# 42 tokens of the last dense tile fetch their experts' rows, where 32 did

## The reference

```python
s1, i1 = lax.top_k(s[:, :, 0], 16); s2, i2 = lax.top_k(s[:, :, 1], 16)      # 8 heads, 128 keys each side
best, pos = lax.top_k(s1[..., None] + s2[..., None, :], 16)                 # 16 experts of a head
gate = softmax(best)
act = einsum('td,thkd->thk', h, expert_u[idx])                              # 8 x 16 = 128 experts a token
out = einsum('thk,thkd->td', gate * gelu(act), expert_v[idx])
```

## Time and profile before

| what | value |
|---|---|
| median of 3 runs | 4116.03 us |
| profiled execution | 4116.04 us, span 4114.3 us |
| PE, PE's weight loads busy | 99%, 90% |
| DVE, ACT, POOL busy | 53%, 34%, 59% |
| experts' units | from about 2058 us |
| value units | from about 3099 us |
| DMA | 929 MB, mean 226 GB/s |

### The profile page before, as it was taken

How to read it: one execution, slowest core, us unless ns; L and a number is a source line. 1 busy time by engine, 2 the same in 40 slices (tenths; PEclk the granted TensorE clock), 3 DMA queues, 4 the chain that set the end, 5 groups by cost and what they waited for, 6 DMA issues and landing times.

```text
span 4114.3 us, 54344 instructions
## 1 busy us (share of the span) xinstructions
PE 4067.4 (99%) x21875; PEld 3688.9 (90%) x21875; DVE 2170.0 (53%) x2854; ACT 1401.8 (34%) x1756; POOL 2420.6 (59%) x768
## 2 busy tenths in 40 slices
PE   8999999999999999999999999999999999999998
PEld 7888888877877888888899999999999999999997
DVE  4300035121122011207888888888437888888885
ACT  4322222332333121223345555555332222232233
POOL 4444443433433434443357777777778888888883
PEclk9999999999999999999999999999999999999999
DMA  4233322222222433323248999999989999999993
GB/s 184 94 123 121 117 102 94 97 82 82 93 82 82 163 115 115 118 92 133 92 165 331 346 345 344 346 347 344 366 340 384 398 381 384 382 385 381 390 364 133
DMA packets 210813, 929.39 MB, mean 226 GB/s; under 512 B 18672, under 2 KB 96816, under 8 KB 111408
## 3 DMA queue, kind: packets, MB, share of 16 engines
q1 hardware_dynamic: 64080, 460.35, 30.4%
q0 software_dynamic: 46080, 335.56, 20.8%
q10 hardware_dynamic: 100576, 132.56, 9.0%
HBM read 864.41 MB, written 64.00 MB: 226 GB/s over the span
## 4 chain that ended last, share of the span: by engine, by line
PE 93%; POOL 2%; DVE 2%; ACT 1%; DMA 1%; issue 1%; ACTq 0%; SPq 0%; DVEq 0%; POOLq 0%
PE bank L1952 16%; PE bank L1953 15%; PE bank L1954 15%; PE bank L1992 8%; PE twin L1992 8%; PE bank L2296 4%; PE twin L2296 4%; PE twin L2298 4%; PE bank L2298 4%; PE twin L2297 4%; PE bank L2297 4%; POOL low L575 1%; PE twin L2267 1%; PE twin L1953 1%; PE twin L1954 1%
## 5 line engine op out<-in xcount | busy, mean ns | idle before, releaser
L575 POOL TENSOR_TENSOR low<-raw,high 128x2048 fp32r<-128x2048 f32 x351 | 1629.2, 4642 | 1447.4 <-ACT high L684 1263.4
L684 ACT ACTIVATE high<-raw 128x2048 fp32r<-128x2048 f32 x190 | 363.9, 1915 | 1220.6 <-PE bank L1954 737.7
L1952 PE MATMUL bank<-x_pack,high 128*128 128x352 f32 x1952 | 630.9, 323 | 8.6 <-POOL low L575 8.6
L1952 PE MATMUL bank<-x_high,high 128*128 128x512 f32 x1632 | 636.9, 390 | 0.0
L1954 PE MATMUL bank<-x_high,low 128*128 128x512 f32 x1632 | 635.0, 389 | 0.0
L1953 PE MATMUL bank<-x_low,high 128*128 128x512 f32 x1632 | 635.0, 389 | 0.0
L1953 PE MATMUL bank<-low_pack,high 128*128 128x352 f32 x1952 | 629.7, 323 | 0.0
L1954 PE MATMUL bank<-x_pack,low 128*128 128x352 f32 x1952 | 629.5, 323 | 0.0
L696 ACT ACTIVATE high<-raw 128x2048 fp32r<-128x2048 f32 x162 | 310.5, 1917 | 737.6 <-PE twin L2298 433.6
L1952 PEld LDWEIGHTS bank<-x_pack,high 128*128 128x128 f32 x1952 | 367.3, 188 | 10.7 <-issue 6.3
L1953 PEld LDWEIGHTS bank<-low_pack,high 128*128 128x128 f32 x1952 | 367.3, 188 | 0.0
(11 more groups left out here) (301 smaller groups left out, 7336.2 us busy)
## 6 DMA issues: line engine op xcount, KB each, us to landing
raw<-weights SPq DMA_DIRECT2D x353, 1024.0 KB
raw_values<-weights SPq DMA_DIRECT2D x42, 1024.0 KB
raw_experts<-weights SPq DMA_DIRECT2D x38, 1024.0 KB
act_dram<-act_out ACTq DMA_DIRECT2D x128, 176.0 KB
retrieved_dram<-stage ACTq DMA_DIRECT2D x44, 512.0 KB
act_in<-act_dram ACTq DMA_DIRECT2D x32, 704.0 KB
gates_in<-retrieved_dram ACTq DMA_DIRECT2D x32, 704.0 KB
gates_dram<-sgu_act ACTq DMA_DIRECT2D x32, 256.0 KB, 2.0
```

The source lines that it names most:

```text
L575: nc.gpsimd.tensor_tensor(low[:, slot, :], rounded, high[:, slot, :].bitcast(F32), ALU.subtract).then_inc(low_done, 1)
L684: nc.scalar.activation(high[:, slot, :], raw[:, slot, :], ACT.Copy).then_inc(high_done, 1)
L1952: nc.tensor.matmul(o, high[:, slot, w], xh, start=(k == 0), stop=False)
```

## The change

`EXTRA` goes from 32 to 42. A token's 128 slots no longer divide evenly: 3 parts of 43 slots, the 129th with gate 0, on 126 partitions; the last two partitions copy the first two of part 0. `EXTRA_GAP` 1 puts an extra row after each slot row, `LATE` goes to 15. The dense part has 342 columns, 86 gate steps, and 11 stages, of which the last has 6 steps and a piece stored after each of the first four. The product of activations and gates is done in two instructions, 10 full stages and 22 columns of the last. The divisor in `sums_by` is 7 units short of the end instead of 10.

```diff
-EXTRA = 32
+EXTRA = 42
-STAGES = COLS // STAGE_TOK
+STAGES = -(-COLS // STAGE_TOK)
+GATE_STEPS = -(-COLS // WTOK)
+LAST_STEPS = GATE_STEPS - STEPS * (STAGES - 1)
+TRAIL = ETILES - FIRST_STEP - GATE_STEPS
-EXTRA_ROWS = SLOTS // EXTRA_SLOTS
-LATE = 16
+EXTRA_ROWS = -(-SLOTS // EXTRA_SLOTS)
+EXTRA_USED = EXTRA_SLOTS * EXTRA
+EXTRA_LISTED = EXTRA_SLOTS * EXTRA_ROWS
+PAD = P - EXTRA_USED
+LATE = 15
-EXTRA_GAP = 2
+EXTRA_GAP = 1
...
-    return min(V_ROWS, early + max(0, unit - begin) * (V_ROWS - LATE) // (ETILES - 10 - begin))
+    return min(V_ROWS, early + max(0, unit - begin) * (V_ROWS - LATE) // (ETILES - 7 - begin))
...
-            act.dma_start(wide_extra[:], extra_x_dram.rearrange("j i d -> (j i) d")).then_inc(extra_x_in, 16)
+            act.dma_start(wide_extra[0:EXTRA_USED, :], extra_x_dram.rearrange("j i d -> (j i) d")).then_inc(extra_x_in, 16)
+            act.dma_start(wide_extra[EXTRA_USED:P, :], extra_x_dram[0, 0:PAD, :]).then_inc(extra_x_in, 16)
...
-                for q in range(STEPS):
+                n_steps, gap = (STEPS, 2) if after else (LAST_STEPS, 1)
+                for q in range(n_steps):
                     expert_unit(q % 2, index + q, high=ring_high)
-                    if before and q % 2 == 0:
-                        keep_stage(s - 1, 1 - half, q // 2)
+                    if before and q % gap == 0 and q // gap < PIECES:
+                        keep_stage(s - 1, 1 - half, q // gap)
...
-                act.dma_start(tile[:], dram.rearrange("j i g -> (j i) g")).then_inc(extra_in, 16)
+                act.dma_start(tile[0:EXTRA_USED, :], dram.rearrange("j i g -> (j i) g")).then_inc(extra_in, 16)
+                act.dma_start(tile[EXTRA_USED:P, :], dram[0, 0:PAD, :]).then_inc(extra_in, 16)
...
+            nc.vector.memset(extra_gates[:, SLOTS:EXTRA_LISTED], 0.0)
...
+            nc.vector.tensor_copy(extra_slots[:, SLOTS:EXTRA_LISTED],
+                                  extra_slots[:, 0:EXTRA_LISTED - SLOTS]).then_inc(extra_named, 1)
...
-                acts = act_in[:, slot, :, :].rearrange("p e (s t) -> p e s t", t=STAGE_TOK)
+                whole = (STAGES - 1) * STAGE_TOK
+                acts = act_in[:, slot, :, 0:whole].rearrange("p e (s t) -> p e s t", t=STAGE_TOK)
                 gates = gates_in[:, slot, :, :, :].rearrange("p s e t -> p e s t")
-                nc.vector.tensor_tensor(acts, acts, gates, ALU.mult).then_inc(product_done, 1)
+                nc.vector.tensor_tensor(acts, acts, gates[:, :, 0:STAGES - 1, :], ALU.mult)
+                acts = act_in[:, slot, :, whole:COLS]
+                nc.vector.tensor_tensor(acts, acts, gates[:, :, STAGES - 1, 0:COLS - whole],
+                                        ALU.mult).then_inc(product_done, 1)
```

More of the change, by code:

```diff
@@ L328, in program @@
         pos_half = c("pos_half", [P, 2, TT, P], U32)
[L329 to L330 removed]
+        extra_slots = at("extra_slots", [P, EXTRA_LISTED], U32, region_b)
+        extra_gates = at("extra_gates", [P, EXTRA_LISTED], F32, region_b + 1024)
         picked = at("picked", [P, P, TOPK], F32, region_b)
@@ L1177, in keep_stage @@
                 if n == 0:
-                    act.wait_ge(step_out, steps.next(STEPS))
+                    act.wait_ge(step_out, steps.next(STEPS if isinstance(s, int) and s < STAGES - 1 else LAST_STEPS))
                 kept_stages[half].next(16)
@@ L1190, in stage_units @@
                 index = s * STEPS + FIRST_STEP
-                for q in range(STEPS):
+                n_steps, gap = (STEPS, 2) if after else (LAST_STEPS, 1)
+                for q in range(n_steps):
                     expert_unit(q % 2, index + q, high=ring_high)
-                    if before and q % 2 == 0:
-                        keep_stage(s - 1, 1 - half, q // 2)
-                    if after or q < STEPS - 1:
+                    if before and q % gap == 0 and q // gap < PIECES:
+                        keep_stage(s - 1, 1 - half, q // gap)
+                    if after or q < n_steps - 1:
                         gate_parts((q + 1) % 2, s * STAGE_TOK + (q + 1) * WTOK)
@@ L1718, in _ @@
             nc.vector.memset(extra_pick[:], 0.0)
-            nc.vector.tensor_copy(extra_gates[:], all_best[:, DENSE_T - 1, :, :].rearrange("p h k -> p (h k)"))
-            nc.vector.scalar_tensor_tensor(out=extra_slots[:], in0=expert_i[:, 0, DENSE_T - 1, :], scalar=float(KEYS),
-                                           in1=expert_i[:, 1, DENSE_T - 1, :], op0=ALU.mult,
-                                           op1=ALU.add).then_inc(extra_named, 1)
+            nc.vector.memset(extra_gates[:, SLOTS:EXTRA_LISTED], 0.0)
+            nc.vector.tensor_copy(extra_gates[:, 0:SLOTS], all_best[:, DENSE_T - 1, :, :].rearrange("p h k -> p (h k)"))
+            then(nc.vector.scalar_tensor_tensor(out=extra_slots[:, 0:SLOTS], in0=expert_i[:, 0, DENSE_T - 1, :],
+                                                scalar=float(KEYS), in1=expert_i[:, 1, DENSE_T - 1, :], op0=ALU.mult,
+                                                op1=ALU.add))
+            nc.vector.tensor_copy(extra_slots[:, SLOTS:EXTRA_LISTED],
+                                  extra_slots[:, 0:EXTRA_LISTED - SLOTS]).then_inc(extra_named, 1)
             dve.wait_ge(gffn_in, 16)
-            dve.wait_ge(extra_x_in, 16)
+            dve.wait_ge(extra_x_in, 2 * 16)
             nc.vector.tensor_tensor(wide_extra[:], wide_extra[:], gffn_all[:], ALU.mult)
@@ L1814, in _ @@
                     dots += 1
-                if at_step < STAGES * STEPS:
+                if at_step < GATE_STEPS:
                     gate_sum(at_step)
@@ L2277, in _ @@
             gate_pair(first=True)
-            with repeat(pe, STAGES * STEPS // 2 - 1, *column_pair, (made, 2), (outs, 2)):
+            with repeat(pe, GATE_STEPS // 2 - 1, *column_pair, (made, 2), (outs, 2)):
                 gate_pair()
```

7 lines of the change are left out of this document (2 added, 5 removed).

## The result

The kernel after takes 4132.01 us (median of 8 runs, 4126.92 to 4138.9), the kernel before, on the same chip, 4118.03 (8 runs): a ratio of 1.003, 95% interval 1.002 to 1.0039. It is slower by 0.3%, where 4100 and a gain of 0.4% was forecast. The profiled execution took 4127.22 us, its span is 4125.5, 11.2 longer than that of before.

What follows compares the result with a forecast made beforehand. Matmul time on TensorE was taken as the bound (PE holds 93% of the chain of waits). -50.8 - 1.0 + 17.5 + 3 + 3 + 0.5 + 11.7 = -16.1 from 4116.03 gave 4100 us, range 4078 to 4120.

Steps and rivals of the forecast that it cites:

- Columns (-50.8): Both stages: 12192 matmuls, each 10 columns narrower, save 4.17 ns each by N + 32 cycles, -50.8 us in all.
- Rival (d): The change doesn't shorten a matmul, 342 columns being charged as 352: 4132 us, slower; chance 0.05.
- Gate steps (-1.0): Gate steps go from 88 to 86, saving two times 0.48 us of PE: -1.0 us.
- Extra rows (+17.5): Experts' stage: slow 2.75 us fetches beside dots with `wide_extra` delay `low`; PE waits 25.3 us against 7.8: +17.5.
- rival (b): Locks cascade: the 13 units with the extra first stall too, +17 more, 4117 us, no change; chance 0.16.
- late-held `low`: Experts' stage: in seven of twelve waits a lone extra's dot keeps `low` late, adding up to 1.25 us each.
- The restart near the end: Behind the wait near the end, TensorE restarts at 1.2 GHz, adding 1.7 us.
- Value stage (+3, +3, +0.5): Value stage: POOL's late `low` +3, late `values` at the entry +3, longer waits behind ACT's table loads +0.5 us.
- The entry: Start of the value stage: two rows a unit outrun the transfers, PE waits for `values`: +3 us (0 to +8).
- POOL's edge: Value stage: with two fetches the next `low` is 0.7 us late against 0.75 slack: +3 (0 to +12).
- Rival (c): Transfers become the value stage's bound, 384 GB/s being the ceiling: +35 us, so 4135, slower; chance 0.09.
- Sums with seven units to go (+11.7): Near the end: the later sum delays ACT's `high` and POOL's `low`; PE waits about 11.2 us, net +11.7.

Runs made afterwards that it cites:

- the bench: TensorE alone with no other work, rows of 96 or 192 matmuls per width in the kernel's order, nothing of the block computed; 342 columns took 157.8 ns at 1536 bytes.
- the lead of 348: Kernel after with 40 tokens (344 columns), extra row first, nine units to go; each experts' unit's first three matmuls take 348 columns: 4090.01 us, ratio 0.9933.

## Why the prediction was wrong

**Columns (-50.8): the step that failed.** "Ten columns are 4.17 ns": measured 2.45 in the experts' stage and 0.88 in the value stage, -20 us for -50.8. These 31 us are the miss: between the profiled executions -16.1 was forecast and +11.2 came, and the other terms, some too high and some left out, end 3 lower together. The bound named for it, 0, was taken for a charge of 342 as 352; that isn't what happened. "Three widths lie on one line" was true of the rows and no ground for a fourth: the bench has up to 5.7 ns more than N + 32 cycles (338) and up to 2.2 less (304), and 352 itself has 160.0 or 161.1 by what runs before it; behind four of 256, as in the kernel, it happens to be the 160.0 of the line. The placement adds to it: at 1368 bytes from row to row 342 columns cost 1.0 more than at the 1408 of before. Rival (d) gave 4132 and the time came out there by luck: it had the columns at nothing instead of -20 and the rows at +4 instead of +12.7, and no wait or clock beyond the forecast ones. Its chance of 0.05 shows how little the assumption was weighed: no row showed a width other than 256, 352 and 512.

**Gate steps (-1.0).** Two of 0.48 us are gone; no run shows them by themselves, they are inside the -13.9.

**Extra rows (+17.5).** Mechanism right: twelve long fetches beside the dot with `wide_extra`, twelve waits, none at the 13 units with the extra first (rival (b) fell). The waits for `low` rose by 12.7: the seven long ones took 1.62 to 2.19 instead of 2.55, the five short ones 1.13 to 1.23 instead of 1.4. The late-held `low` was overrated. Two experiments, one on each kernel, took the waits away by the order of rows alone. That the long fetches "contradict" the inference on descriptor generation goes further than the runs: they show the fetch held up, not which part of it.

**The clock (not in the sum but for one restart).** The restart near the end was priced at 1.7 and cost 1.8. Three more falls, of some 1.5 us each, had no term: a wait of 2 to 3 us was taken to cost itself only. One of them is in the experts' stage and belongs to the price of the extra rows.

**A wait that wasn't forecast (3.4).** ACT's store issue and a later GELU, in the units behind the last gate step:

```profile
2913.95 4.32 ACTq L1131 DMA_DIRECT2D act_dram<-act_out  x1
...
2937.12 0.46 ACT L1126 ACTIVATE act_out<-bank 128x342 f32<-128x342 f32 x1 [8.39 <-DMA act_dram<-act_out]
```

The forecast had put the four pieces stored in successive units at nothing; the kernel before stores its last four so as well and had no such wait. Whether they or the general load on the DMA engines held this store wasn't tried; the kernels with the extra first had waits of 3 to 4.5 us near this place in some profiles and none in others.

**Value stage (+3, +3, +0.5).** The entry was sized right: at unit 16 of the stage 9.7 us had been lost beyond the pitch, before 6.2, so +3.4, of which the lower clock is 1.5. The waits for `values` sum to 5.8 only because two later ones of the kernel before (at 3347, and the 1.18 of the earlier trace rows) are gone; at the entry they rose from 4.1 to 5.8. POOL's edge and the second instruction of the product cost nothing: 0.1 us lost from unit 16 to 117. That holds for a unit of 7.62 us. At 7.47, near the forecast 7.48, the kernel before with 340 columns loses 7.8 there, so the edge was no false alarm; the longer unit may have hidden it. The two waits behind ACT's table loads grew by 0.25 together. Rival (c) fell: from 3200 to 4000 the kernel after moved 392 GB/s, and with the lead of 348 in the experts' stage 403 from 3600 to 3700, so 384 was no ceiling.

```profile
3200.00:4000.00 800.00, 800.00 (x5038) 799.99 (x5037) 696.94 (x660) 232.99 (x133) 693.77 (x263) 1.00 0.99 392
```

**Sums with seven units to go (+11.7).** Right: 10.82 of wait, twelve matmuls 282 to 287 ns apart and one 448 behind it, for 1.8, less the 1.18 of the earlier trace rows, +11.4. Taking it back gives 7 in the trace, since the same rows in fewer units cost waits for `values` elsewhere.

## What to carry to other kernels

The pitch of back-to-back matmuls is not a smooth function of the columns: measure the exact width, at the exact distance of rows and with what runs ahead of it, in a bench of a few hundred matmuls, before a change of layout is paid for; here the bench gave the kernel's units to 0.01 us. Four columns at the right place are worth as much as ten at the wrong one: 340 columns were 24 us faster than 344, 342 were 22 faster than 352, and 344 no slower than 342. (340 columns were run on the kernel before with part of the result left out. As a change of `EXTRA` they need 44 tokens, and three parts of 44 don't fit on 128 partitions.) A wait can cost more than its length: look at the granted clock behind it. Where a slow instruction of one engine overlaps another's, look first at the order of the two: the same rows in another order gave back 10 us before and 22 after (13 of them between the two profiled executions).

## What the runs showed of the hardware

- Back-to-back fp32r matmuls settle into a repeating pattern: 156, 158, 159 ns or 153, 153, 154 at 344 columns, kept over 96 and 192 matmuls and over changes of the PSUM bank. Which one, the widths just before decide, and not by being wider or narrower: three of 348 give the fast one, three of 352 to 384 don't, twelve of 352 do.
- A pitch can lie under N + 32 cycles: 153.33 at 344 columns, where that would be 156.67, and 131.7 at 288, where it would be 133.3.
- Where the moving operand's columns begin counts as well: 342 columns, 384 from row to row, 157.7 from column 0, 153.3 from columns 2 and 8, 156.7 from column 10 (once each, behind 340 columns; from column 0 also behind seven other widths). So does the distance of rows: 158.84 at 1368 bytes, 156.70 at 1376, 157.83 at 1408.
- At 192 and at 128 columns the pitch was 111.6 and 111.5, so less than 192 columns brought nothing.
- Behind waits of 2.07, 2.69 and 2.8 us the granted clock fell to 0.50 for ten to twelve matmuls, at some 1.5 us each; behind other waits of 2.07 to 2.19 it didn't.
- An indirect fetch that takes 0.94 us beside the dot product with `wide` (PSUM) is held up beside the one with `wide_extra`, where DVE reads two SBUF operands: it ends 0.81 us after that instruction does, whether it lasts 2.75 us for that or 2.38. It was so with all eight fetches in the kernel before and all twelve after that began inside such a dot, and not with the 24 and 31 inside whose last third such a dot began (1.23 us each); so it may be the order of the two that counts. The Trainium skill, SBUF — State Buffer, section Who interferes with whom, infers of a `tensor_tensor` with both inputs in SBUF that it leaves descriptor generation alone. Beside this SCALAR_TENSOR_TENSOR the fetches are held up all the same; as they also take their row numbers from SBUF (`slot_i`, `extra_i`), the runs don't tell whether it is that read or the making of descriptors that waits.
- What sets the phase of a pattern, and why only part of the kernel's units take the lead of 348, stays open.
